# Two softmax attentions: scores two units ahead issued behind the values, maps finished a unit early, output transposes moved ahead of the next values

## The chip, the core and the metric

The kernel runs on one core of one Trainium2 chip. Its time is the device time of one execution, in microseconds (us). The core has a matrix engine (TensorE, PE in the rows, its weight loads PEld), a vector engine (VectorE, DVE), an activation engine (ScalarE, ACT), a general engine (GpSimd, POOL) and a queue that here only issues DMAs (SyncE, SP). Each engine works through its own instructions in the order in which they were written, and semaphores hold an instruction until another engine has done its part. So an instruction that waits also holds all that stands behind it on its engine.

## The reference

Two model blocks over 512 tokens and width 1024. The first (a state-space scan, dilated attention, a gated FFN) is not touched. The second has two layers, and the change is in their attentions and a little around them. Layer A, differential attention with 8 heads; layer B, forgetting attention with 16 heads of 64:

```python
# A: per head, per block of 128 queries, keys up to the block's end
logits = einsum(q[:, q0:q0+128], k[:, :k_end]) + bias      # two maps per head
p = softmax(logits)
attn = p[:, 0] - lam * p[:, 1]
o = rms_norm(einsum(attn, v[:, :k_end]), subln_g) * (1 - lambda_init)
...
# B: c is the running sum of log forget gates
logits = einsum(q[:, q0:q0+128], k[:, :k_end]) + c[t] - c[s]
o = einsum(softmax(where(dist >= 0, logits, NEG_INF)), v[:, :k_end])
...
# after each attention: h = h + rms_norm(f), f = conv_ffn(rms_norm(h))
u = causal_conv_width_3(x @ w_in) + conv_b
gate, val = split(u)
f = (gelu(gate) * val) @ w_out
```

## The kernel before

All large products are float32 to nearly full precision, made from three products of rounded parts (high times high, low times high, high times low). GpSimd splits each slab of weights into its two parts ahead of its use: a slab is two chunks of 128 rows by 256 columns (`whi`, `wlo`), four slabs make a panel of 1024 rows, and four slabs at most are ready ahead. A slab is 12 products of 512 columns on TensorE (L634), or 24 of 256 columns where the result is wanted token by token (the values v2 and v3, L628). The two PSUM banks of a panel are freed when VectorE has copied its result out (`evicted`), called "epi" in the lists below.

Each attention has 32 units, u = 0 to 31: unit u is head tile u//4 and query block u%4, so its width is 128, 256, 384 or 512 keys. The function `order2` (L232) writes one list of steps, and all engines go through that one list, each taking its own part of a step. The steps of a unit:

- S (TensorE, L948): both score maps into AUX banks 0 and 1; waits until VectorE has read the maps of the unit before (`sc_ready`).
- M: VectorE adds the bias and takes the maximum (L2019, L2022), ScalarE does the two exponentials (L1358). In layer B the bias row `negc` comes by DMA from `c_dram`.
- D (VectorE): reciprocals (L2029); in layer A also the difference of the two maps into `dif` (L2033, L2036).
- T: TensorE transposes `dif` (A) or `sc` (B) (L987), ScalarE copies the result to `pT` (L1368), and in B VectorE copies the second half (L2026). T waits until ScalarE has read the last output transpose (`oT_ready`).
- V (TensorE, L1002 in A, L997 in B): values. W: VectorE scales them into `osb2` (L2050 or L2046); in A ScalarE squares them (L1372).
- Y, layer A only, once per tile of four units: ScalarE takes the square root (L1375), which needs another activation table than the exponential, and VectorE normalizes the tile (L2053, L2055).
- X, once per tile: TensorE transposes the tile's output (L968), ScalarE copies it to `oT` (L1378). In the last units O rounds it into `opA_hi` (ScalarE, L1382) and `opA_lo` (VectorE, L1438).

Between these steps stand the slabs of the next pair's q, k and v panels (12 for 8 units), in the last 8 units six slabs of the output projection. Before the change one unit of layer A reads: M(u+1), T(u), S(u+2), W(u-1), D(u+1), slab, V(u), slab. Y and X of a tile come in the second and the third unit of the next tile (u%4 = 1 and 2). Seven products of a mask with an identity (`keep_warm`, L735) stand ahead of T at u = 0, 1, 24 and 25.

Layer B begins with a projection of the forget gates ("f"): narrow transposes, a softplus on ScalarE and VectorE (`sp_step`, ending in L2088), running sums on TensorE (L1031), a copy and a DMA to `c_dram` (L1409), and the load of `negc`. TensorE does three slabs of q3 before it waits for the softplus, and the fourth after the sums.

The FFN of each layer (`fin`, L1924 on) runs over 11 pairs of panels. VectorE copies a panel out of PSUM (L1935), and does two convolution taps per tile (L1945), the product with the gate (L1952) and the low part (L1956).

## Time and profile before

| | us |
|---|---|
| median of 3 runs (2549.43 to 2551.54) | 2551.06 |
| the profiled execution | 2551.49 |
| its span, first to last instruction | 2549.7 |
| TensorE busy | 2484.7 (97%) |
| VectorE busy | 1314.8 (52%) |
| ScalarE busy | 748.1 (29%) |
| GpSimd busy | 1617.3 (63%) |
| mean granted TensorE clock | 0.993 |

Layer A's attention runs from about 1238 to 1443 us of the span, layer B's from about 1899 to 2131. The times of instructions are from one execution. A matmul's recorded time is longer than its share of the engine, since matmuls overlap: 12 products of 512 columns, each recorded with 0.39 us, pass in about 2.8 us. A row's last bracket gives the idle time of the engine just before the instruction and what ended it. Where the granted clock is 1.00 the matrix engine runs at its upper level, 2.4 GHz; where it is 0.50 at the lower one, 1.2 GHz.

### The profile page before, as it was taken

Reading aid. Unit: us, or ns where it says so; the run is one execution under the profiler, and the core shown is the slowest. Engines: PE = TensorE matmul, PEld = TensorE weight load, DVE = VectorE, ACT = ScalarE, POOL = GpSimd, SP = SyncE. Lnnn points to the kernel's source line nnn. Section 1 sums busy time; section 2 is a strip of 40 time slices with the busy share of each in tenths; the row PEclk is TensorE's granted clock in tenths of the full one; section 3 lists DMA queues with packets and bytes.
Section 4 is the critical chain, followed back from the end, with each engine's and each line's share of the span. In section 5 each row is a group of like instructions: output and inputs, shape, how many; then the busy total and the mean of one; then the engine's idle time right before and its main releaser. Section 6 shows DMA issues by size and latency. Waiting matters only on the chain. (4 is left out here: it accounts for less than half of the span.)

```text
span 2549.7 us, 37097 instructions
## 1 busy us (share of the span) xinstructions
PE 2484.7 (97%) x12731; PEld 2054.1 (81%) x12744; DVE 1314.8 (52%) x2044; ACT 748.1 (29%) x1396; POOL 1617.3 (63%) x1548
## 2 busy tenths in 40 slices
PE   9999999999999999999999899999989999999998
PEld 7888898888778888888787677888867777878886
DVE  8778675435226333302555468773173344787722
ACT  3564551011232111102244434331032222433300
POOL 8765666755447777776543368887653324778874
PEclk9999999999999999999999999999999999999999
DMA  5433434322224333332321123333222212333331
GB/s 163 128 101 92 114 100 133 97 71 71 67 66 124 96 98 95 96 98 83 105 65 58 50 83 93 97 95 100 78 85 71 71 59 66 84 90 98 95 99 62
DMA packets 235792, 229.22 MB, mean 90 GB/s; under 512 B 15809, under 2 KB 228289, under 8 KB 235673
## 3 DMA queue, kind: packets, MB, share of 16 engines
q1 hardware_dynamic: 212224, 204.72, 28.0%
q10 hardware_dynamic: 23448, 22.84, 3.0%
q8 instruction: 83, 1.36, 0.2%
q14 instruction: 37, 0.30, 0.0%
HBM read 225.29 MB, written 4.84 MB: 90 GB/s over the span
## 5 line engine op out<-in xcount | busy, mean ns | idle before, releaser
L594 POOL TENSOR_TENSOR wlo<-raw,whi 128x512 fp32r<-128x512 f32 x772 | 1056.7, 1369 | 64.5
L592 POOL TENSOR_SCALAR whi<-raw 128x512 fp32r<-128x512 f32 x772 | 562.4, 728 | 841.8 <-issue 446.9
L634 PE MATMUL PS<-opA_hi,whi 128*128 128x512 f32 x1872 | 745.0, 398 | 11.8 <-DVE fu L1935 4.3
L634 PE MATMUL PS<-opA_hi,wlo 128*128 128x512 f32 x1872 | 730.9, 390 | 0.0
L634 PE MATMUL PS<-opA_lo,whi 128*128 128x512 f32 x1872 | 730.3, 390 | 0.0
L634 PEld LDWEIGHTS PS<-opA_hi,whi 128*128 128x128 f32 x1872 | 352.6, 188 | 98.7 <-issue 14.9
L634 PEld LDWEIGHTS PS<-opA_hi,wlo 128*128 128x128 f32 x1872 | 352.1, 188 | 75.0
L634 PEld LDWEIGHTS PS<-opA_lo,whi 128*128 128x128 f32 x1872 | 352.8, 188 | 70.3 <-issue 1.2
L1945 DVE SCALAR_TENSOR_TENSOR facc<-fu,vec,facc 128x512 f32<-128x512 f32 x176 | 206.2, 1230 | 44.9 <-ACT facc L1330 44.6
L628 PE MATMUL PS<-whi,opA_hi 128*128 128x256 f32 x704 | 205.7, 292 | 0.0
L628 PE MATMUL PS<-wlo,opA_hi 128*128 128x256 f32 x704 | 198.9, 283 | 0.0
L628 PE MATMUL PS<-whi,opA_lo 128*128 128x256 f32 x704 | 198.9, 283 | 0.0
L634 PE MATMUL PS<-hid_hi,whi 128*128 128x512 f32 x480 | 186.7, 389 | 0.0
L634 PE MATMUL PS<-hid_lo,whi 128*128 128x512 f32 x480 | 186.7, 389 | 0.0
L634 PE MATMUL PS<-hid_hi,wlo 128*128 128x512 f32 x480 | 186.7, 389 | 0.0
L628 PEld LDWEIGHTS PS<-whi,opA_hi 128*128 128x128 f32 x704 | 134.6, 191 | 7.5 <-issue 4.7
L628 PEld LDWEIGHTS PS<-whi,opA_lo 128*128 128x128 f32 x704 | 134.7, 191 | 1.4 <-issue 1.2
L628 PEld LDWEIGHTS PS<-wlo,opA_hi 128*128 128x128 f32 x704 | 134.6, 191 | 0.0
L1900 DVE COPY branch<-PS 128x512 f32<-128x512 f32 x32 | 21.0, 687 | 210.0 <-PE PS L634 147.9
L1358 ACT ACTIVATE sc<-sc,bstat 128x128 f32<-128x128 f32 (+3 forms) x128 | 70.8, 554 | 117.3 <-DVE bstat L2022 117.3
L634 PEld LDWEIGHTS PS<-hid_hi,wlo 128*128 128x128 f32 x480 | 90.1, 188 | 18.8
L634 PEld LDWEIGHTS PS<-hid_hi,whi 128*128 128x128 f32 x480 | 90.1, 188 | 18.7
(306 smaller groups left out, 3310.7 us busy)
## 6 DMA issues: line engine op xcount, KB each, us to landing
raw<-in_w_in_dram SPq DMA_DIRECT2D x184, 256.0 KB, 2.8
raw<-in_ffn_w_in_dram SPq DMA_DIRECT2D x176, 256.0 KB, 2.7
raw<-in_ffn_w_out_dram SPq DMA_DIRECT2D x88, 256.0 KB, 2.8
raw<-in_a_w_qkv_dram SPq DMA_DIRECT2D x48, 256.0 KB, 2.7
raw<-in_w_ffn_gate_dram SPq DMA_DIRECT2D x44, 256.0 KB, 2.8
raw<-in_w_ffn_up_dram SPq DMA_DIRECT2D x44, 256.0 KB, 2.7
raw<-in_w_ffn_down_dram SPq DMA_DIRECT2D x44, 256.0 KB, 2.9
acs_row<-acs_dram ACTq DMA_DIRECT2D x16, 512.0 KB, 5.6
```

The source lines that it names most:

```text
L592: nc.gpsimd.tensor_scalar(whi[slot][:], raw[raw_slot][:], 1.0, 1.0, ALU.mult, ALU.mult).then_inc(w_high, 1)
L594: nc.gpsimd.tensor_tensor(wlo[slot][:], raw[raw_slot][:], whi[slot][:].bitcast(F32), ALU.subtract).then_inc(slab_split, 1)
L628: last = nc.tensor.matmul(psum_tm(key, panel)[:, t, :], a, b[:, c, :], start=t % 2 == 0 and k + n == 0, stop=k == total - 1 and n == 2, sk ...
L634: last = nc.tensor.matmul(psum_fm(key, panel, m), a, b[:, k, :], start=k + n == 0, stop=k == total - 1 and n == 2)
L1358: A(sc[:, u % 2, e, 0:width], sc[:, u % 2, e, 0:width], ACT.Exp, bias=bstat[:, u % 4, 2 + e:3 + e], accum_out=bstat[:, u % 4, 4 + e:5 + e] ...
L1900: V.tensor_copy(branch[:, c, :], psum_fm(key, c // 2, c % 2)).then_inc(evicted, 1)
L1945: V.scalar_tensor_tensor(facc[:, j, :], fu[:, j, tap:tap + S], col("ffn_conv_w_2", 132 * l + 44 * tap + FT * half + m + 2 * i), facc[:, j, ...
```

## The change

- `order2` is rewritten. One unit of layer A now reads: T(u), D(u+1), slab, V(u), W(u), S(u+2), M(u+2), slab. So the scores of u+2 stand behind the values of u, and the exponentials of u+2 stand ahead of the copy to `pT` of u+1. The two halves of the old step Y are now Y (ScalarE's square root, behind W of the tile's last unit) and Z (VectorE's normalization, behind D(u+1) of the next unit); the two halves of O are O and L. X stands directly ahead of V of the next tile's first unit, and in layer A it waits for Z.
- X also waits for the copy of the transposes just ahead of it, since it stands behind T now.
- The first two slabs of the next pair stand between S(0) and S(1).
- `keep_warm` is issued at u = 24 and 25 only.
- In layer B all four slabs of q3 stand ahead of the running sums, TensorE's wait for `c_ready` is at T(0), and the copy of v3 out of PSUM stands ahead of the softplus on VectorE.
- In `fin`, VectorE copies the next pair's first panel out between the taps of the two halves.
- ScalarE does one small copy at the very start.

```diff
--- before.py
+++ after.py
@@ -232,49 +232,45 @@
 def order2(names):
     project = "awo" if names[0] == "q2" else "bwo"
-    out = [("S", 0), ("S", 1), ("M", 0), ("D", 0)]
-    late = []
+    out, late = [("S", 0), ("M", 0), ("D", 0)], []
     for j in range(PAIRS):
         fill = [("slab", (n, j + 1), 0, h) for n in names for h in range(4)] if j < PAIRS - 1 else []
-        for n in range(9, len(fill) + 3, 2):
+        if j == 0:
+            out += fill[:2] + [("S", 1), ("M", 1)]
+            fill = fill[2:]
+        for n in range(9 - 2 * (j == 0), len(fill) + 3, 2):
             fill.insert(n, None)
         if j == PAIRS - 1:
             fill = [None] * 2 + [("slab", project, n, k) for k in range(3) for n in range(2)]
         for u in range(8 * j, 8 * j + 8):
-            if u < 31:
-                out.append(("M", u + 1))
-            out += [("W", u - 1)] * (u > 0 and names[0] == "q3") + [("T", u)]
-            if u < 30:
-                out.append(("S", u + 2))
-            out += [("W", u - 1)] * (u > 0 and names[0] != "q3")
+            done = u // NB - 1
+            out.append(("T", u))
             if u < 31:
                 out.append(("D", u + 1))
+            if u % NB == 0 and u and names[0] == "q2":
+                out.append(("Z", done))
+            if u > 24:
+                out.append(("L", u - 25))
             out += late
             late = []
-            done = (u - 5) // NB
-            if u % NB == 1 and u > NB and names[0] == "q2":
-                out.append(("Y", done))
             for part in ("V", "X"):
-                if part == "X" and u % NB == 2 and u > NB:
-                    out.append(("X", done))
                 if fill and (j < PAIRS - 1 or part == "X"):
                     t = fill.pop(0)
                     out += [t] * (t is not None)
                     if t is not None and t[1] != project and t[3] == len(K1024) - 1:
                         late = [("epi", t[1], t[2])]
                 if part == "V":
-                    out.append(("V", u))
+                    out += [("X", done)] * (u % NB == 0 and u > 0) + [("V", u), ("W", u)]
+                    if u % NB == NB - 1 and names[0] == "q2":
+                        out.append(("Y", u // NB))
+                    if u < 30:
+                        out += [("S", u + 2), ("M", u + 2)]
             if u in range(24, 31):
                 out.append(("O", u - 24))
-    return out + [("W", 31)] + [("Y", 7)] * (names[0] == "q2") + [("X", 7), ("O", 7)]
+    return out + [("Z", 7)] * (names[0] == "q2") + [("X", 7), ("O", 7), ("L", 7)]
 WEIGHTS = ["w_in", "w_ssm_out", "w_att_out", "w_mix_out", "w_ffn_gate", "w_ffn_up", "w_ffn_down", "a_w_qkv_2", "a_w_o_2", "w_kvf_2",
            "b_w_q_2", "b_w_o_2", "ffn_w_in_2_0", "ffn_w_in_2_1", "ffn_w_out_2_0", "ffn_w_out_2_1"]
@@ -429,7 +425,7 @@
         AUX = ctx.enter_context(nc.psum_tensor("AUX", [P, 4, S], F32))
         x_in = [sem(f"x_in{n}") for n in range(4)]
-        warm_ready = sem("warm_ready")
+        warm_ready, table_ready = sem("warm_ready"), sem("table_ready")
         first_in, const_in = sem("first_in"), sem("const_in")
         w_loaded = [sem(f"w_loaded{n}") for n in range(RAW)]
         slab_go, w_high, slab_split = sem("slab_go"), sem("w_high"), sem("slab_split")
@@ -962,8 +958,10 @@
                     elif kind == "X":
                         if fox:
                             pe.wait_ge(o2_read, 32 + 8 * (u + 1))
+                            pe.wait_ge(pT2_dve, min(NB * u + NB + 1, 32))
                         else:
                             pe.wait_ge(o2_normed, u + 1)
+                            pe.wait_ge(pT2_act, min(NB * u + NB + 1, 32))
                         for n in range(NB):
                             last = nc.tensor.transpose(AUX[:, 2 + fox, n * P:(n + 1) * P], osb2[:, u % 2, n, :], ident[:])
                         last.then_inc(ot2_done, 1)
@@ -974,7 +972,9 @@
                         U = u_base + u
                         if kind == "T":
                             wait(pe, oT_ready, tiles)
-                            if u % (8 * (PAIRS - 1)) < 2:
+                            if fox and u == 0:
+                                pe.wait_ge(c_ready, 1)
+                            if u in (24, 25):
                                 keep_warm(WARM_UNIT, 2 + fox)
                             if fox:
                                 wait(pe, exp2, 2 * U + 2)
@@ -1021,8 +1021,7 @@
             twin_mm(("k3", 0), 7)
             factors_between(7, ("v3", 0), 0)
             narrow_transposes("f", f_rows, BH)
-            for k in range(3):
-                slab(("q3", 0), 0, k)
+            panel_mm(("q3", 0), 0)
             pe.wait_ge(sp_step, 33)
             for t in range(NB):
@@ -1030,8 +1029,6 @@
                 for n, (part, x) in enumerate(sums):
                     last = nc.tensor.matmul(AUX[0:BH, 2, t * P:(t + 1) * P], x, part[:], start=n == 0, stop=n == len(sums) - 1)
             last.then_inc(c_done, 1)
-            slab(("q3", 0), 0, 3)
-            pe.wait_ge(c_ready, 1)
             attention(("q3", "k3", "v3"), 1)
             for n in range(2):
                 slab("bwo", n, 3)
@@ -1080,6 +1077,9 @@
                 A(std[:], AUX[:, 3, 0:NB], ACT.Sqrt, bias=EPS, scale=1.0 / D).then_inc(std_ready, 1)
+            act.wait_ge(warm_ready, 1)
+            A(std[:], rstd_bc[:, 0:NB], ACT.Copy).then_inc(table_ready, 1)
+            act.wait_ge(table_ready, 1)
             act.wait_ge(first_in, 16 * N_FIRST)
             for c in range(DC):
                 act.wait_ge(x_in[c // 2], 16)
@@ -1969,9 +1969,9 @@
                 evict(1, 1)
                 with dve.Fori(1, FP - 1) as i:
                     taps(i, 0)
-                    taps(i, 1)
                     dve.wait_ge(fconv_tap, 88 * l + 8 * i + 4)
                     evict(i, 0, 1)
+                    taps(i, 1)
                     products(i)
                     evict(i, 1, 1)
                 taps(FP - 1, 0)
@@ -2035,7 +2035,7 @@
                             wait(dve, tr2_done, u - 1)
                             V.scalar_tensor_tensor(dif[:, u % 2, 0:width], sc[:, u % 2, 1, 0:width], st[:, 10:11], sc[:, u % 2, 0, 0:width],
                                                    ALU.mult, ALU.add).then_inc(r2_step, 1)
-                    elif kind == "O":
+                    elif kind == "L":
                         low(opA_lo[:, u, :], oT[:, u, :], None, opA_hi[:, u, :])
                     elif kind == "W":
                         wait(dve, ot2_done, 8 * fox + tile - 1)
@@ -2048,7 +2048,7 @@
                         else:
                             dve.wait_ge(pv2_done, u + 1)
                             V.tensor_scalar(osb2[:, tile % 2, qb, :], AUX[:, 3, 0:P], st[:, 6:7], None, ALU.mult).then_inc(o2_read, 1)
-                    elif kind == "Y":
+                    elif kind == "Z":
                         dve.wait_ge(o2_std, u + 1)
                         V.reciprocal(ostat[:, u % 2, 2 * NB:3 * NB], ostat[:, u % 2, NB:2 * NB]).then_inc(o2_rstd, 1)
                         dve.wait_ge(o2_rstd, u + 1)
@@ -2082,11 +2082,11 @@
             opB_low(7)
             scale_first(("k3", 0), k_first)
             narrow_columns(fx, bfv[:], 2, BH)
+            qkv2(("v3", 0))
             step, q, a = softplus((fa, fe, fr, fz, fz2, fq), 18, 3)
             step(V.scalar_tensor_tensor(fz[:], q[:], 2.0, a[:], ALU.mult, ALU.add))
             step(V.tensor_tensor(fr[:, 2, :], fz[:, 0, :], fz[:, 1, :], ALU.add))
             step(V.tensor_tensor(fr[:, 3, :], fr[:, 2, :], fz[:, 2, :], ALU.add))
-            qkv2(("v3", 0))
             qkv2(("q3", 0))
             softmax_units(("q3", "k3", "v3"), 1)
             residual("bwo", 8, "b_norm_post_2", 0, ("ffn_norm_pre_2", 8), 2, (("fin", 1), fu_first))
```

In the instruction streams of the engines this looks as follows. The first place is ScalarE in layer A, where the first tile has ended: the square root with its table (L1375), the exponentials (L1358), the copies to `pT` (L1368), the squares (L1372) and the copy of the transposed output (L1378). Before:

```order
L1372 ACTIVATE osq,ostat<-osb_164 128x128
L1375 ACT_TABLE_LOAD
L1375 ACTIVATE ostat<-ostat 128x4
L1358 ACT_TABLE_LOAD
L1358 ACTIVATE sc,bstat<-sc,bstat 128x512 x2
L1368 ACTIVATE pT<-AUX 128x384
L1372 ACTIVATE osq,ostat<-osb_164 128x128
L1378 ACTIVATE oT<-AUX,subg 128x512
```

and now:

```order
L1372 ACTIVATE osq,ostat<-osb_164 128x128
L1375 ACT_TABLE_LOAD
L1375 ACTIVATE ostat<-ostat 128x4
L1358 ACT_TABLE_LOAD
L1358 ACTIVATE sc,bstat<-sc,bstat 128x256 x2
L1368 ACTIVATE pT<-AUX 128x128
L1378 ACTIVATE oT<-AUX,subg 128x512
```

The square root stood one unit and more behind the tile's last square and three instructions ahead of the output copy; now it follows the last square directly, and the output copy comes after one exponential and one copy to `pT`.

The same place on VectorE: reciprocals (L2029), the difference (L2033, L2036), the normalization (L2053, L2055) and the scaled values (L2050). Before:

```order
L2029 RECIPROCAL bstat<-bstat 128x2
L2033 TENSOR_SCALAR bstat<-bstat,lams 128x1
L2036 SCALAR_TENSOR_TENSOR dif<-sc,bstat 128x384
L2053 RECIPROCAL ostat<-ostat 128x4
L2055 TENSOR_TENSOR osb_164<-osb_164,ostat 128x512
```

and now:

```order
L2029 RECIPROCAL bstat<-bstat 128x2
L2033 TENSOR_SCALAR bstat<-bstat,lams 128x1
L2036 SCALAR_TENSOR_TENSOR dif<-sc,bstat 128x256
L2053 RECIPROCAL ostat<-ostat 128x4
L2055 TENSOR_TENSOR osb_164<-osb_164,ostat 128x512
L2050 TENSOR_SCALAR osb_164<-AUX,bstat 128x128
```

The normalization now stands behind the difference of width 256, whose exponentials follow the two table loads above; before it stood behind the difference of width 384, whose exponentials came before them.

On TensorE, the output transposes (the x4 row) and what is around them. Before:

```order
L628 MATMUL PS<-whi_59,opA_lo 128x256
L628 MATMUL PS<-wlo_63,opA_hi 128x256
L1002 MATMUL AUX<-v_0_158,pT 128x128 x3
L968 MATMUL AUX<-ident,osb_164 128x128 x4
L987 MATMUL AUX<-ident,dif 128x128 x4
L948 MATMUL AUX<-k_1_157,q_1_155 128x256 x2
```

and now (the numbers of lines are four or two lower there for the same code):

```order
L624 MATMUL PS<-wlo_62,opA_hi 128x256
L966 MATMUL AUX<-ident,osb_164 128x128 x4
L1002 MATMUL AUX<-v_0_158,pT 128x128
L944 MATMUL AUX<-k_0_156,q_0_154 128x384 x2
L987 MATMUL AUX<-ident,dif 128x128 x2
```

They stood behind the values of the next tile's third unit and stand now ahead of the values of its first, and the scores follow the values.

## Rows read from the trace of the kernel before

**Rows 1.** Busy time by stretch, layer A's attention: length, engines, clock, DMA share, GB/s.

```profile
1238.00:1440.00 202.00, 187.42 (x1062) 146.25 (x1065) 108.29 (x337) 88.32 (x258) 80.03 (x84) 0.97 0.18 54
```

**Rows 2.** Waits of TensorE around layer A's attention: waiter, awaited, us, times, longest.

```profile
PE AUX L1002 <- ACT pT L1368: 6.0, 4, 3.8
PE AUX L948 <- DVE bstat L2019: 4.5, 2, 3.1
PE AUX L987 <- ACT oT L1378: 2.3, 3, 0.8
```

**Rows 3.** The same view around layer B's attention.

```profile
PE AUX L987 <- DVE osb L2046: 7.2, 9, 1.5
...
PE AUX L987 <- ACT oT L1378: 2.1, 3, 0.7
```

**Rows 4.** ScalarE in time order, layer A: start us, us, engine, line, operation.

```profile
1328.87 0.30 ACT L1372 ACTIVATE osq<-osb 128x128 f32<-128x128 f32 x1
...
1329.28 1.28 ACT L1375 ACT_TABLE_LOAD   x1
1330.58 0.20 ACT L1375 ACTIVATE ostat<-ostat 128x4 f32<-128x4 f32 x1
1330.80 1.28 ACT L1358 ACT_TABLE_LOAD   x1
...
1341.36 0.51 ACT L1358 ACTIVATE sc<-sc,bstat 128x256 f32<-128x256 f32 x1 [0.95 <-DVE bstat L2022]
```

**Rows 5.** VectorE in time order, layer A.

```profile
1331.03 0.69 DVE L2055 TENSOR_TENSOR osb<-osb,ostat 128x512 f32<-128x512 f32 x1
...
1344.20 0.35 DVE L2050 TENSOR_SCALAR osb<-AUX,bstat 128x128 f32<-128x128 f32 x1 [2.87 <-PE AUX L1002]
1344.46 0.16 DVE L2029 RECIPROCAL bstat<-bstat 128x2 f32<-128x2 f32 x1
...
1344.96 0.67 DVE L2036 SCALAR_TENSOR_TENSOR dif<-sc,bstat 128x256 f32<-128x256 f32 x1
```

**Rows 6.** The chain that ended last: seven mask products, a slab, a slab of values.

```profile
1913.34 1.53 PE AUX L735 x7
1916.58 2.82 PE PS L634 x12
...
1941.67 2.93 PE PS L628 x24
```

**Rows 7.** TensorE in time order, layer A: scores of width 256.

```profile
1316.79 0.70 PE L948 MATMUL AUX<-k,q 64*128 64x256 f32 x4
```

**Rows 8.** Widest maps, layer A: one of two bias passes, one of two exponentials.

```profile
1304.74 0.68 DVE L2019 CUSTOM_DVE_ANT_0 sc<-AUX,tbias 128x512 f32<-128x512 f32 x1
...
1405.09 0.72 ACT L1358 ACTIVATE sc<-sc,bstat 128x512 f32<-128x512 f32 x1 [1.18 <-DVE bstat L2022]
```

**Rows 9.** Busy time by stretch, columns as in rows 1: TensorE's clock after idle time.

```profile
1402.00:1404.00 2.00, 0.00 (x0) 0.00 (x0) 1.84 (x4) 1.89 (x3) 0.00 (x0) 1.00 0.00 0
1404.00:1406.00 2.00, 0.80 (x4) 0.50 (x4) 1.28 (x6) 0.91 (x3) 0.00 (x0) 0.53 0.00 0
...
1432.00:1434.00 2.00, 2.00 (x10) 1.90 (x10) 0.12 (x1) 0.35 (x1) 0.00 (x0) 0.50 0.00 0
```

**Rows 10.** The start of layer B's attention in time order.

```profile
1901.42 0.29 DVE L2019 CUSTOM_DVE_ANT_0 sc<-AUX,negc 128x128 f32<-128x128 f32 x1 [2.08 <-DMA negc<-c_dram]
...
1901.99 0.79 PE L948 MATMUL AUX<-k,q 64*128 64x256 f32 x4 [1.84 <-DVE bstat L2019]
...
1905.88 0.39 PE L987 MATMUL AUX<-ident,sc 128*128 128x128 f32 x2
```

**Rows 11.** The first FFN's second pair of panels, VectorE and TensorE in time order.

```profile
1541.89 4.93 DVE L1945 SCALAR_TENSOR_TENSOR facc<-fu,vec,facc 128x512 f32<-128x512 f32 x4 [2.49 <-ACT facc L1330]
...
1548.27 0.47 PE L634 MATMUL PS<-opA_hi,whi 128*128 128x512 f32 x1 [2.14 <-DVE fu L1935]
```

**Rows 12.** TensorE at the kernel's start.

```profile
11.18 0.51 PE L634 MATMUL PS<-opA_hi,whi 128*128 128x512 f32 x1 [0.18 <-POOL wlo L594]
```

## The prediction

> **What bounds the kernel now.** I read the page first: TensorE is busy for 97% of the span, so only its idle time and its clock can be won, some 65 us in all. The waits of TensorE say where that time lies, and the stretches say how much of it the two attentions hold: layer A's attention has 202.0 - 187.4 = 14.6 us of idle time at a mean clock of 0.97 [rows 1]. In A the longest waits are for the copies to `pT` and for the maps ahead of scores [rows 2]; nearly all lie in the last 8 units, where few slabs are left to cover a chain over three engines. In the 24 units before them TensorE waits only 0.8 us per two tiles, for the copy of the output. In B it waits for the scaled values (8 times 0.72 us in the body, once 1.5 in the end) and for the output copy [rows 3]. Then I went through the instructions in time order, for the price of each step, and walked the new list by hand, one engine beside the other, with these prices.
>
> **The prices.** Square 0.41 (start to the next load), first table load to second 1.52, second load 1.28, exponentials of width 256 about 1.1 (two of 0.5 with their sums) [rows 4]. Scaled values 0.35, reciprocal to difference 1.17, normalization 0.69 and about 0.2 for its reciprocal [rows 5]. A slab 2.82, a slab of values 2.93, seven mask products 1.5 [rows 6]. Scores of width 256 hold TensorE 0.6, the widest 1.1 [rows 7]. Widest maps: 1.5 on VectorE, 1.5 on ScalarE [rows 8].
>
> **Layer A, the body.** X of a tile now waits for Z, Z stands behind D(u+1) on VectorE, D(u+1) waits for the exponentials of u+1, and these follow both table loads on ScalarE. From the end of V of a tile's last unit: hand-over 0.1, W 0.35, square 0.41, load to load 1.52, load 1.28, exponentials 1.10, difference 1.17, normalization 0.90, further hand-overs 0.15: 6.98 us until X can start. Meanwhile TensorE has S 0.63, T 0.2 and one slab of 2.93, 3.8 in all: a wait of 3.2 us. That is tile 0. At tile 1 VectorE copies a value panel out ahead of W (4.1); tile 3 gives 3.3; at tiles 2 and 4 a second slab leaves 0.4 each. Sum 11.4. Besides, V of a unit now waits for a copy to `pT` that stands behind the exponentials of the next unit: 1.9 once and three times 0.4, 3.1 in all. Removed: three waits of 0.8 for the output copy [rows 2] and 0.3 of small ones. Body: 11.4 + 3.1 - 2.6 = +11.9. Queued behind X are V, the next scores and all slabs, so nothing covers this.
>
> **Layer A, the end.** Before, the waits from u = 25 on sum to 11.9 us, most of them in [rows 2]. Now X of tile 5 has no slab ahead of it, only S, T and the mask products: 6.98 - 2.5 = 4.5. X of tile 6 has one: 3.3. Where no slab stands between, V(u) to V(u+1) takes the widest scores 1.1, the map 1.5, the exponentials 1.5 [rows 7, 8], the rounding for the output and a copy, about 5.5, against 1.6 of TensorE's own work: 3.9 at the worst, 2.2 at V(25) behind the mask products, and 0.7 to 1.2 at four others, with 0.8 at the last X, 10.4 in all. Sum 18.2, so +6.3.
>
> **Layer A, the entry.** Scores of unit 0 start as before, at 1238.0. T(0) came 5.7 us later; now S 0.4, two slabs and S(1) 0.6 make 6.6, with no wait. +0.9, two slabs fewer later (-5.6), and no mask products at T(1) (-1.5): -6.2.
>
> **The clock.** After 2 us without any matmul, and little before, the granted clock falls from 1.00 to 0.5 [rows 9]. It did so twice in A's end, for about 7 and about 3.5 us, which is 3.4 and 1.7 us of work lost. The change makes six idle stretches of 3.2 us or more, three in the body. I take 1.5 for each of the three, since slabs follow, and 1.1 for each of the three in the end, where TensorE waits anyway: 7.8 against 5.1 before, +2.7. The unknown has as ends nothing (-5.1) and 3.4 each (+15.3).
>
> Layer A: 11.9 + 6.3 - 6.2 + 2.7 = **+14.7**.
>
> **Layer B.** The fourth slab of q3, 2.82 us [rows 6], goes into the wait for the softplus, which is a little shorter; the running sums start 0.3 later, and the load of `negc` with them. The copy of v3, 1.7 us, goes into VectorE's wait for ScalarE's first exponential, at no cost; if it did not fit it would be 1.7. The first map starts when `negc` has landed, 1901.42 before and 1901.7 now, and frees S(1) at 1902.3, against 1901.99 [rows 10]. S(1) takes 1.0, and T(0) comes at 1903.4 instead of 1905.9, since no mask products stand ahead of it: -2.5. The two slabs between S(0) and S(1) cover the load of `negc` but for 0.5 and are done by then, -5.6. The mask products of T(1) go: -1.5. In the body 5.8 of 0.72s and 2.1 of output copies go [rows 3], 2.1 come back as waits for `pT`: -5.7. There is no Z here, so X waits only for copies. In the end the waits rise from about 5 to about 9.5 by the chain of layer A's end: +4.5, and one of them, 3.7, should cost a clock step: +1.7. Layer B: **-9.1**.
>
> **The FFN.** VectorE's copy came behind two pairs of taps, the second of which is 4.93 us, and TensorE waited 2.14 us for it, once in each FFN [rows 11]. Now it falls into VectorE's own wait of 2.49. In the later pairs the copy must wait for TensorE's panel with the taps behind it; VectorE has about 5 us of slack in the 22 of a pair, and TensorE needs the result one panel later. -4.3, bounds -4.3 and 0.
>
> **The start.** The early copy takes the table load off the way to the first matmul. TensorE's second slab still waited for GpSimd [rows 12], so what is won comes back as that wait: -0.1, bounds -1.3 and 0.
>
> **The sum.** 14.7 - 9.1 - 4.3 - 0.1 = +1.2, so 2552.7 by the profiled execution's 2551.49. This is 0.4 above the median of the runs; by the median it is 2552.3, and I say 2552.5.
>
> What counts as a change that can be told from none is 0.2% of the time, 5.1 us.
>
> One rule speaks against this change. The two loads around the square root cost 1.52 us from the start of one to the start of the other, and the square root itself starts 1.30 after the first load's start [rows 4]. The Trainium skill (ScalarE: Activation LUTs, What ACT_TABLE_LOAD costs) puts 1283 ns for the load and about 1380 ns for a drain on every switch. By that rule two switches in each of seven chains, of which before only the last was exposed, would add an estimated 17 to 19 us, and the sum would be near 2571. The trace does not agree: no drain stands between load and square root.
>
> **The rivals.**
>
> *The clock decides (slower).* Each of the six stretches costs what the first one before did, 3.4 us, instead of 1.3: +12.6, 2565. For it: in [rows 9] the lower level outlasted the wait by 4 us, and at half speed the engine's small steps in A's end are late for the next chain too. Against it: in the body slabs follow at once. From 2.0 us a stretch on, the kernel is slower by more than 0.2%.
>
> *The normalization is not what X waits for (faster).* V of the same unit waits for a copy behind the same exponentials, 5.1 us after the last V, so 1.3 of wait stay in any case. If Z were through by then, as when D is not in its way, five waits shrink by 1.9 and the clock mostly stays up: -9.5 and about -1.5, 2541.5. For it: before, Z came between two maps without holding anyone. Against it: Z now stands behind D of width 256, which needs the exponentials behind the loads.
>
> *Layer B's entry gives nothing (slower).* The load of `negc` or the split weights are late, TensorE waits out what the two slabs should cover: +5.6, 2558. For it: `negc` was 2.1 us late for VectorE [rows 10]. Against it: TensorE waited there for vectors and loads alone, for no weights, and GpSimd may be four slabs ahead.
>
> *The change does not do what it says.* The maps are a unit early only by their place; if the chain through them sets the pace in the body as well, every unit with one slab loses about 1 us, 12 in A and B each, 2575. V's small waits of 0.4 in my walk bound this from below.
>
> **The numbers.** Forecast 0.42, the clock 0.28, the normalization 0.20, B's entry 0.06, the pace of the chain 0.04. The forecast's own range is 2546 to 2558, and its upper tail beyond 2556.2 counts as slower. Faster 0.22, same 0.42, slower 0.36. The range 2542 to 2566 leaves out the third loss and half of the gain's tail.
>
> **What would show it.** In the changed trace: waits of TensorE at the output transposes for VectorE's normalization, seven of them in A, near 3, 4, 0.4, 3, 0.4, 4.5 and 3 us; half clock after the long ones; no wait at T in the body of either attention; T(0) of B 2.5 us earlier, counted from the sums, with two slabs ahead of it; no wait on L1935. The forecast is wrong if the waits at X are under 1.5 us, or if the clock's share in A is above 12 us, or if B gains under 5.

## The result and the profile after

The changed kernel takes 2561.25 us (median of 5 runs, 2560.33 to 2564.17), the kernel before 2551.53 us on the same chip. The ratio is 1.0043, 95% interval [1.0029, 1.0057]: the change costs 9.7 us. The forecast was 2552.5.

I cut both executions at the same three instructions: the first scores of layer A's attention, its last output transposes, and the last output transposes of layer B's. The view is busy time by stretch, with the columns of [rows 1]. Before:

```profile
core 0: us, PE busy (x) PEld busy (x) DVE busy (x) ACT busy (x) POOL busy (x), PEclk, DMA share, GB/s
1238.03:1442.71 204.68, 189.49 (x1071) 147.56 (x1073) 109.13 (x339) 90.01 (x261) 80.45 (x85) 0.97 0.19 55
1442.71:2130.24 687.53, 663.21 (x3422) 539.99 (x3427) 355.96 (x620) 193.97 (x352) 424.71 (x400) 1.00 0.28 82
2130.24:2549.70 419.46, 404.68 (x1799) 331.98 (x1799) 239.98 (x255) 113.89 (x149) 303.77 (x278) 0.98 0.30 87
```

The same three stretches of the changed kernel:

```profile
1238.01:1464.23 226.22, 195.95 (x1057) 150.45 (x1059) 106.87 (x339) 92.34 (x261) 83.99 (x85) 0.93 0.16 50
1464.23:2144.09 679.86, 662.58 (x3410) 543.64 (x3414) 373.34 (x620) 192.89 (x352) 424.07 (x400) 0.99 0.27 83
2144.09:2559.50 415.41, 402.73 (x1799) 330.75 (x1799) 254.72 (x255) 113.92 (x149) 302.64 (x278) 0.99 0.29 88
```

| stretch | forecast | measured | TensorE's idle time | its busy time |
|---|---|---|---|---|
| layer A's attention | +14.7 | +21.5 | +15.1 | +6.5 |
| first FFN and layer B | -11.2 | -7.7 | -7.0 | -0.6 |
| second FFN | -2.1 | -4.1 | -2.1 | -2.0 |

The spans differ by 9.8 us, and the three rows add up to it. Read the last two columns together. In A the changed kernel has 14 instructions of TensorE fewer (mask products, some 4.1 us of it), and is busy 6.5 us longer all the same: the engine ran at its lower clock for longer.

Where A waits now (waits of TensorE, columns of [rows 2]):

```profile
PE AUX L966 <- DVE osb L2055: 19.2, 8, 4.4
PE AUX L1002 <- ACT pT L1368: 9.5, 10, 3.6
PE AUX L1002 <- issue: 1.5, 2, 1.0
```

The first row is new. It is the output transposes waiting for the normalization, at 3.31, 3.64, 0.37, 3.31, 0.36, 4.35, 3.19 and 0.64 us in order of time. The forecast had 3.2, 4.1, 0.4, 3.3, 0.4, 4.5, 3.3 and 0.8. The waits of scores for `bstat` and of the map's transposes for `oT` [rows 2] are gone.

The forecast's chain can be read off in tile 5, in time order over three engines:

```profile
1405.98 0.35 DVE L2050 TENSOR_SCALAR osb<-AUX,bstat 128x128 f32<-128x128 f32 x1 [1.68 <-PE AUX L1002]
...
1406.36 0.31 ACT L1372 ACTIVATE osq<-osb 128x128 f32<-128x128 f32 x1 [2.48 <-DVE osb L2050]
...
1406.78 1.28 ACT L1375 ACT_TABLE_LOAD   x1
1408.08 0.21 ACT L1375 ACTIVATE ostat<-ostat 128x4 f32<-128x4 f32 x1
1408.30 1.28 ACT L1358 ACT_TABLE_LOAD   x1
1409.60 0.51 ACT L1358 ACTIVATE sc<-sc,bstat 128x256 f32<-128x256 f32 x1
...
1410.72 0.17 DVE L2029 RECIPROCAL bstat<-bstat 128x2 f32<-128x2 f32 x1 [3.19 <-ACT sc L1358]
...
1411.63 0.17 DVE L2053 RECIPROCAL ostat<-ostat 128x4 f32<-128x4 f32 x1
1411.84 0.69 DVE L2055 TENSOR_TENSOR osb<-osb,ostat 128x512 f32<-128x512 f32 x1
...
1412.58 1.11 PE L966 MATMUL AUX<-ident,osb 128*128 128x128 f32 x4 [4.35 <-DVE osb L2055]
```

From the scaled values to the transposes it is 6.60 us, of which 2.82 is from the start of the first table load to the end of the second. VectorE sits idle for 3.19 us with the normalization queued behind the difference. The square root starts 1.30 us after its load, as in [rows 4]: no drain. The Trainium skill (ScalarE: Activation LUTs, What ACT_TABLE_LOAD costs) has a drain of about 1380 ns with every switch; the trace after does not show it either, and the 2571 us that would follow from it were not reached.

What the forecast had wrong shows in the clock behind such waits, by stretch:

```profile
1300.00:1304.00 4.00, 2.39 (x10) 1.38 (x10) 1.83 (x5) 1.09 (x3) 0.12 (x1) 0.76 0.24 70
1304.00:1308.00 4.00, 4.00 (x17) 3.04 (x16) 2.11 (x8) 1.31 (x4) 0.00 (x0) 0.82 0.00 0
...
1356.00:1360.00 4.00, 2.94 (x11) 1.44 (x11) 1.96 (x6) 1.09 (x3) 0.00 (x0) 0.58 0.19 65
1360.00:1364.00 4.00, 4.00 (x12) 3.18 (x11) 2.27 (x8) 1.30 (x4) 0.00 (x0) 0.56 0.00 0
...
2104.00:2108.00 4.00, 2.88 (x14) 2.76 (x14) 0.86 (x2) 1.07 (x4) 0.00 (x0) 0.52 0.00 0
2108.00:2112.00 4.00, 4.00 (x16) 3.13 (x17) 1.16 (x7) 1.40 (x5) 0.00 (x0) 0.62 0.00 0
```

The first two pairs are in layer A, the third in B. 4 us times the missing share of the clock gives (0.24 + 0.18) x 4 = 1.7 us for the first pair, 3.4 for the second and for the third. Over A six stretches add up to 15.4 us (1.7, 1.7 and 3.4 in the body, 3.4, 3.4 and 1.7 in the end) where the kernel before had 6.8 in three. This sum also counts time in which TensorE stood idle at the lower level, and lost no work. Weighted with its busy share in steps of 0.5 us, it is 13.5 against 5.6.

In layer B (waits of TensorE from 1905 us on):

```profile
PE AUX L997 <- ACT pT L1368: 4.4, 2, 3.4
PE AUX L997 <- DVE pT L2026: 3.7, 5, 0.9
PE AUX L997 <- issue: 1.7, 2, 1.2
PE AUX L944 <- DVE bstat L2019: 1.5, 1, 1.5
PE AUX L966 <- DVE pT L2026: 0.9, 2, 0.5
PE AUX L987 <- ACT sc L1358: 0.9, 1, 0.9
```

The 7.2 us at the scaled values and the 2.1 at the output copies of [rows 3] are gone; at the values (L997) 9.8 us stand where there were 2.6.

### The profile page after: what moved, and what is told of

The parts are those of the page before. It is cut to its first block, busy times and chain, and to the rows that moved or that the text cites. A ratio compares the mean times of both kernels' runs of the same rounds, so it can differ in the third digit from the quotient of the medians.

```text
span 2559.5 us, 37062 instructions
## 1 busy us (share of the span) xinstructions
PE 2488.7 (97%) x12705; PEld 2059.3 (80%) x12716; DVE 1344.5 (53%) x2044; ACT 749.8 (29%) x1397; POOL 1620.0 (63%) x1548
## 4 chain that ended last, share of the span: by engine, by line
PE 87%; DVE 6%; ACT 4%; issue 2%; DMA 0%; ACTq 0%; DVEq 0%
PE PS L630 64%; PE PS L624 9%; PE PS L703 3%; PE AUX L944 2%; PE AUX L997 1%; DVE opA_lo L1440 1%; PE AUX L910 1%; PE AUX L891 1%; ACT opA_hi L1073 1%; PE AUX L987 1%; PE AUX L848 1%; DVE XT L1920 1%; PE AUX L1002 1%; ACT sc L1358 1%; PE AUX L737 0%
## 5 line engine op out<-in xcount | busy, mean ns | idle before, releaser
L630 PEld LDWEIGHTS PS<-opA_hi,whi 128*128 128x128 f32 x1872 | 353.1, 189 | 96.9 <-issue 13.2
L1945 DVE SCALAR_TENSOR_TENSOR facc<-fu,vec,facc 128x512 f32<-128x512 f32 x176 | 216.7, 1289 | 15.8 <-ACT facc L1330 15.8
L1358 ACT ACTIVATE sc<-sc,bstat 128x128 f32<-128x128 f32 (+3 forms) x128 | 70.9, 555 | 184.1 <-DVE bstat L2022 184.0
L630 PEld LDWEIGHTS PS<-hid_lo,whi 128*128 128x128 f32 x480 | 90.1, 188 | 18.7
```

The source lines that it names most:

```text
L630: last = nc.tensor.matmul(psum_fm(key, panel, m), a, b[:, k, :], start=k + n == 0, stop=k == total - 1 and n == 2)
L1358: A(sc[:, u % 2, e, 0:width], sc[:, u % 2, e, 0:width], ACT.Exp, bias=bstat[:, u % 4, 2 + e:3 + e], accum_out=bstat[:, u % 4, 4 + e:5 + e] ...
L1945: V.scalar_tensor_tensor(facc[:, j, :], fu[:, j, tap:tap + S], col("ffn_conv_w_2", 132 * l + 44 * tap + FT * half + m + 2 * i), facc[:, j, ...
```

## The experiments

The ratios are to the kernel before, timed beside each experiment, whose median was 2550.4 to 2550.9 us.

**One part back: layer A in the old order.** The changed kernel with the old list for layer A alone, and the mask products at units 0 and 1 there.

```diff
 def order2(names):
     project = "awo" if names[0] == "q2" else "bwo"
+    if names[0] == "q2":
+        return order2_old(names)
...
-                            if u in (24, 25):
+                            if u in (24, 25) or not fox and u < 2:
```

> Layer A's attention takes the order of before (with the mask products at units 0 and 1), all else is the changed kernel. Theory (the loss sits in A alone: its attention took 21.5 us longer, from scores of unit 0 to the last output transpose, while B and the two FFNs gained): the time falls by 21.5, from 2561.3 to about 2539.8, 11.7 under the kernel before. Rival (part of the loss comes from outside A's attention, from the clock or from weights that are late elsewhere): over 2545.

Measured: 2539.35 us (2538.35 to 2539.98), ratio 0.9955 [0.9941, 0.9968]. So layer A's new order costs 21.9 us, and all else in the change wins 11.5 (their difference is 10.4 and not 9.7, since the kernel before was 0.7 lower beside this run). The sign of the whole is decided in one attention.

**The idle time filled.** The changed kernel with mask products, read by nobody, ahead of the first seven output transposes of layer A: 14, 14, 2, 14, 2, 18 and 14.

```diff
+                            if u < 7:
+                                pe.wait_ge(o2_read, NB * (u + 1))
+                                keep_warm((14, 14, 2, 14, 2, 18, 14)[u], 3)
                             pe.wait_ge(o2_normed, u + 1)
```

> The changed kernel, with mask products into a free bank ahead of each of the first seven output transposes of A (14 each where the wait was over 3 us, 18 at tile 5, 2 at tiles 2 and 4), so that the matrix engine has work while it waits. The waits for the normalization keep their length. Theory (each long wait costs a stretch at half clock of 3.4 or 6.8 us besides, 1.7 to 3.4 us of work, and this comes on top of the wait): the granted clock stays at 1.00 in the body of A, and the time falls by 7 to 10, to 2551 to 2554. Rival (the slow stretches lie beside other waits and cost little): 2559 to 2562.

Measured: 2554.14 us (2552.30 to 2557.75), ratio 1.0016 [1.0007, 1.0025], 7.1 less than the changed kernel though nothing that TensorE waits for comes earlier. Layer A's attention:

```profile
PE AUX L1005 <- ACT pT L1371: 10.8, 10, 3.6
PE AUX L969 <- DVE osb L2058: 2.2, 6, 0.7
...
sum 218.51, PE 203.07 PEld 152.84 DVE 109.28 ACT 92.25 POOL 83.82; mean PE 203.07 PEld 152.84 DVE 109.28 ACT 92.25 POOL 83.82
```

Idle time falls from 30.3 to 15.4, and 78 mask products at the 0.219 us each of [rows 6] add 17.1; yet the engine's busy time rises by only 7.1. The other 10.0 us are the lower clock that was avoided. The mechanism held; the time is a tenth above the range expected of it.

**The transposes later.** X of layer A one unit later, ahead of the values of the next tile's second unit.

```diff
-                    out += [("X", done)] * (u % NB == 0 and u > 0) + [("V", u), ("W", u)]
+                    out += [("X", done)] * (u % NB == late_x and u > NB - 1) + [("V", u), ("W", u)]
...
-                            pe.wait_ge(pT2_act, min(NB * u + NB + 1, 32))
+                            pe.wait_ge(pT2_act, min(NB * u + NB + 2, 32))
```

> The changed kernel with A's output transposes one unit later (ahead of the values of the tile's second unit, u%4 = 1, instead of the first). The square root, its tables and the normalization stay where they are. Theory (the output transposes wait for the normalization behind the difference behind the table loads; a unit later the 7.0 us chain is over): the seven waits of 19.2 in all go, V of the first unit keeps a wait of about 1.3 us for its copy where one slab stands ahead, 5 in all, and the clock stays up in the body: 14 + 7 less, about 2540. Rival (the new place of scores and maps sets the pace by itself, the transposes only show it): the wait moves to the values, 2550 or more.

Measured: 2554.59 us (2553.28 to 2555.88), ratio 1.0014 [1.0005, 1.0023]. The time is the rival's (2550 or more), 14 us above the theory's. No wait at X for the normalization is left but 0.7 us at the last tile, yet the waits have moved to the values: those for `pT` sum to 13.2, and two more appear at the values of units 16 and 24, one 4.93 and one 5.97 us. Around the first, in time order:

```profile
1349.45 0.69 DVE L2056 TENSOR_TENSOR osb<-osb,ostat 128x512 f32<-128x512 f32 x1
1350.06 1.65 DVE L1706 TENSOR_SCALAR v<-PS,rstd_col 128x256 f32<-128x256 f32 x4
...
1351.81 0.76 PE L1003 MATMUL AUX<-v,pT 128*128 128x128 f32 x2 [4.93 <-issue]
```

The trace names no releaser, but VectorE's copy of the value panel out of PSUM ends at 1351.71, and the values, which need that panel, start 0.10 later. In its list the copy stands behind the normalization, and so behind the same two table loads. The next experiment tests this.

**The copy ahead.** As the last, and the copy of a panel stands ahead of the difference.

```diff
+            if late_x:
+                out += late
+                late = []
             if u < 31:
                 out.append(("D", u + 1))
```

> As e3_x_late (the output transposes of the first attention a unit later), and the copy-out of the value panels stands ahead of the next unit's masks' division in VectorE's list, not behind it. Theory (the waits of 4.9 and 6.0 us at the 16th and 24th unit's values in e3_x_late came from that copy-out, which stood behind the division and so behind the two table loads): both waits go, and with them their clock: 2554.6 - 10.9 - about 4 = 2540. Rival: those values wait for something else, or the division now comes late for the transposes: 2550 or more.

Measured: 2544.54 us (2541.64 to 2546.05), ratio 0.9973 [0.9964, 0.9983]. Both waits are gone, and the time is 10.1 us less; in the traces layer A has 10.5 less (220.1 to 209.6). The cause was right, the size expected (2540) was not reached. Layer A is still 6.5 us longer than in the first experiment (203.1). It now waits here:

```profile
PE AUX L1006 <- ACT pT L1372: 16.6, 13, 3.6
PE AUX L970 <- ACT pT L1372: 3.3, 3, 2.1
```

The copies to `pT` stand behind the next unit's exponentials. Waits for them sum to 6.0 before [rows 2], to 19.9 here; in return some 7 us of the old order's waits, for `bstat` and `oT` [rows 2], are gone. No experiment changes the place of the exponentials alone, so how this remainder divides stays open. Nor was the normalization tried ahead of the difference, the nearest cure for the 19.2 us.

**No table to switch.** The changed kernel with a square in place of the square root in layer A's second attention. It leaves the root out of the normalization.

```diff
-                        A(ostat[:, u % 2, NB:2 * NB], ostat[:, u % 2, 0:NB], ACT.Sqrt, bias=SUB_EPS, scale=1.0 / P).then_inc(o2_std, 1)
+                        A(ostat[:, u % 2, NB:2 * NB], ostat[:, u % 2, 0:NB], ACT.Square, scale=1.0 / P).then_inc(o2_std, 1)
```

> The changed kernel, with the square root of A's normalization replaced by a square, so that no activation table is loaded between the exponentials. It leaves the square root out. Theory (the loads are 2.6 of the 7.0 us chain, no drain besides): waits at the output transposes of 3.3 become 0.7, 4.4 becomes 1.8, the short ones go, 19.2 becomes 5; with the clock up, about 22 less, 2539. Rival (a switch costs a drain of some 1.4 us each besides, as the Trainium skill has it): the chain is 5.3 shorter, no wait is left there, and about 27 is won, 2534.

Measured: 2545.62 us (2539.93 to 2547.55), ratio 0.9976 [0.9965, 0.9986]. Layer A's attention:

```profile
PE AUX L1002 <- ACT pT L1368: 9.6, 10, 3.6
PE AUX L966 <- DVE osb L2055: 7.5, 5, 2.3
...
1238.19:1444.64 206.45, 187.27 (x1057) 145.48 (x1059) 109.53 (x339) 73.47 (x246) 85.61 (x84) 0.98 0.18 54
```

This is the cleanest comparison of the study. TensorE issues the same 1057 instructions as in the changed kernel; its idle time is 11.1 us less, and its busy time 8.7 us less. So here 1 us less of waits brought 0.8 more in clock. The time came out 6.6 us above what I expected, for two reasons. Each long wait at the transposes shrank by only 1.9 to 2.4 us, so 7.5 are left and not 5; tile 5's, 4.35 in the changed kernel, is the longest. And this execution, 19.8 us shorter in layer A, is only 16.0 shorter in all: up to the last output transposes of B TensorE is busy 3.6 us longer, with the clock down also from 1476, 1845 and 1957 us on, behind waits of only 0.19, 0.19 and 1.06. The times fall in two groups, two runs near 2540 and six at 2545 to 2548. The rival's drains did not show: the waits shrank by less than the 2.8 us of the two loads, not by 5.3.

```profile
1397.44 0.65 PE L966 MATMUL AUX<-ident,osb 128*128 128x128 f32 x4 [2.33 <-DVE osb L2055]
```

So at this tile the rest of the chain, some 4.2 us, is by itself longer than the work that TensorE has beside it.

**The FFN alone.** The kernel before, with its copy between the taps.

```diff
                     taps(i, 0)
-                    taps(i, 1)
                     dve.wait_ge(fconv_tap, 88 * l + 8 * i + 4)
                     evict(i, 0, 1)
+                    taps(i, 1)
```

> The kernel before with one edit alone: in the feed-forward stages the eviction that follows the last product's group is put between the taps, and so the two stages' ends no longer wait 2.14 us on the last hidden rows. My theory: each of the two stages gets shorter by 2.1 to 2.2 us (it did in the changed kernel: 2.15 and 2.1), so -4.3 us, about 2547. Rival: the stage's end is hidden behind something else that is late when it comes earlier, the time stays at 2551 (above 2550).

Measured: 2544.43 us (2542.41 to 2548.84), ratio 0.9979 [0.9969, 0.9989]: 5.9 us less, more than the two waits. In the changed kernel the second FFN is shorter by 4.1 us for one wait of 2.13. The execution of the kernel before shows what can come on top, around that wait, which ended at 2236.85 (busy time by stretch):

```profile
2234.00:2238.00 4.00, 1.87 (x7) 1.25 (x6) 4.00 (x5) 0.09 (x1) 3.08 (x3) 0.87 0.20 66
2238.00:2242.00 4.00, 4.00 (x14) 3.11 (x14) 3.62 (x6) 3.80 (x5) 0.38 (x1) 0.70 0.21 66
```

The clock fell there: (0.13 + 0.30) x 4 = 1.7 us. In the first FFN it stayed at 1.00 after a wait of 2.14 [rows 11], and that FFN's share was 2.1, as forecast. That the 1.6 us beyond the forecast, in the median of runs from 2542 to 2549, are this clock is likely but not shown by one execution.

**Layer A's entry alone.** The first experiment with the change's start of layer A: two slabs between S(0) and S(1), no mask products.

```diff
-    out = [("S", 0), ("S", 1), ("M", 0), ("D", 0)]
+    out = [("S", 0), ("M", 0), ("D", 0)]
...
+        if j == 0:
+            out += fill[:2] + [("S", 1)]
+            fill = fill[2:]
```

> e1_a_old (the first attention in the order of the kernel before, all else changed) with the changed kernel's beginning of that attention: two slabs of the value weights' products between the first two scores, no mask products there. Theory (the entry's term of the forecast, -6.2 with clock, of which part was lost to the clock): 2539.4 - 4 = about 2535. Rival: the gap at the entry comes back at the first transposes, 2539 or more.

Measured: 2535.76 us (2534.70 to 2537.40), ratio 0.9942 [0.9929, 0.9956]: 3.6 us below the first experiment and the fastest kernel of the study, 15 us below the one before and 25 below the changed one. From the first scores to T(1) it takes 14.41 us against 12.86, with two more slabs (5.6) done: 4.1 us won. The forecast had 6.2 for this. It read the entry off an execution in which the clock was low there; with the same old list, the first experiment has it at 1.00. This kernel has the changed one's entry, so it prices the rest of the new order: 25.5 us in the times, 24.9 in A (226.2 against 201.3), and 8.3 of it are left with the copy ahead (209.6).

**Layer B's slab back.** The first experiment with the slab of q3 where it was before: three slabs, the sums, the fourth slab. All else that the change does at layer B's start stays: the copy of v3, the place of S(1), and no mask products.

```diff
-            panel_mm(("q3", 0), 0)
+            for k in range(3):
+                slab(("q3", 0), 0, k)
...
             last.then_inc(c_done, 1)
+            slab(("q3", 0), 0, 3)
```

> e1_a_old with the second attention's beginning as in the kernel before: three slabs, the sums, then the fourth slab, in place of all that the change does there. Theory (the first transposes wait less for the map behind the slab, forecast at -2.5 us in the changed kernel): 2539.4 + 2.5 = about 2542. Rival: the place of the slab is worth nothing, since the scores' wait for the statistics (1.5 us) takes its place: 2539.4 within 1 us.

Measured: 2539.67 us (2538.46 to 2542.23), ratio 0.9955 [0.9941, 0.9968], 0.3 from the first experiment, whose runs overlap with these. The rival was right: moving the slab is worth nothing that can be measured. The traces show how. With the slab back TensorE waits 2.46 us ahead of the sums and 1.45 ahead of S(0); in the first experiment it waits 1.45 for `bstat` at S(1) and 0.98 for the exponentials at T(0), 1.5 less in all. But there the clock is at 0.76 and 0.82 between 1900 and 1908 us, 1.7 us of work, while it stays at 1.00 with the slab back.

**The end kept busy.** The fastest kernel (layer A's entry alone) with 12 mask products ahead of the scores of unit 28 and 16 ahead of the values of unit 30 of layer A.

```diff
+                        if u == 28 and not fox:
+                            pe.wait_ge(o2_read, 26)
+                            keep_warm(12, 3)
                         scores(u)
...
+                            if u == 30 and not fox:
+                                pe.wait_ge(o2_read, 30)
+                                keep_warm(16, 3)
```

> e7_a_old_entry with products that nobody reads in the two long idle stretches near the end of the first attention: 12 mask products ahead of the scores of unit 28, which waited 3.07 us, and 16 ahead of the values of unit 30, which waited 3.83 us. At 0.21 us each they last 2.5 and 3.4 us and fit into the waits. Theory (an idle stretch costs its own length and then some 1.7 to 3.4 us of work at the lower clock): the waits' ends stay, the clock stays at 1.00 in both places, and the time falls by about 4 to 5 us, from 2535.8 to about 2531. Rival (the clock falls anyway, or the lower clock costs nothing because the work behind it is hidden): 2535 or more.

Measured: 2537.62 us (2537.09 to 2538.49), ratio 0.9949 [0.9936, 0.9963], 1.9 slower than without them. A miss, and a telling one. TensorE around unit 30 without the products:

```profile
1423.34 0.49 PE L1031 MATMUL AUX<-ident,dif 128*128 128x128 f32 x3
1427.65 1.20 PE L1046 MATMUL AUX<-v,pT 128*128 128x128 f32 x6 [3.83 <-ACT pT L1412]
...
1433.25 0.60 PE L1031 MATMUL AUX<-ident,dif 128*128 128x128 f32 x4
```

and with them:

```profile
1423.61 0.49 PE L1034 MATMUL AUX<-ident,dif 128*128 128x128 f32 x3
1426.25 3.63 PE L775 MATMUL AUX<-mask,ident_bf 128*128 128x512 bf16 x16 [2.15 <-DVE osb L2100]
1429.71 0.83 PE L1052 MATMUL AUX<-v,pT 128*128 128x128 f32 x6
...
1433.58 0.60 PE L1034 MATMUL AUX<-ident,dif 128*128 128x128 f32 x4
```

The products had to wait for their bank, 2.15 us, and so ran past the end of the wait: the values start 2.06 us later. But 4 us on, at the next transposes, only 0.33 of this is left, 0.27 of which was there before: the clock, at 1.00 from 1428 to 1432 us against 0.57 without the products, gave back 1.7. At unit 28 they came after 3.54 us of idle time, at half clock, and took 4.45. From the transposes ahead of them to the next it is 12.84 us, against 11.81 without: 1.0 lost. The clock's price is confirmed, the filling as placed is not worth it.

## Why the prediction was off, point by point

The forecast's signs held for all three stretches but not its sizes, and the time, 2561.25, lies outside the forecast's own range (2546 to 2558) and within the wide one, which takes in most of what the clock was thought able to cost. Of the three outcomes, the one given 0.36 came (slower by more than 0.2%), not the one given 0.42. The time is nearer to the rival in which the clock decides (2565) than to the forecast (2552.5). One of the prediction's own signs of being wrong appeared: the clock's share in A above 12 us (15.4, or 13.5 where only busy time counts). The other two did not.

- *The body and the end of A: right.* The waits at the transposes sum to 19.2 us against 20.0 by the walk, and those at the values to 11.0 against 12.7. All idle time of A rose by 15.1 us; the terms of the forecast, without clock and mask products, give 16.0.
- *The clock's term of A: the step that failed.* +2.7 was forecast. Measured is the rise of busy time, 6.5, and the 4.1 of mask products that went: about +10.5 (by the stretches with a low clock it is 8.6, or 7.9 weighted with busy time). The average over the six stretches is 15.4 / 6 = 2.6 us, where I took 1.5 and 1.1 (7.8 in all), on the argument that slabs follow in the body and that TensorE waits anyway in the end. The runs show neither saves: in the body 1.7, 1.7 and 3.4 us were lost with slabs right behind, in the end 3.4, 3.4 and 1.7, of which 2.5, 3.0 and 1.7 are busy time. The prediction named 2.0 as the point from which the kernel is slower by more than 0.2%. Two experiments show that this is clock and not work: 10.0 us came back with the idle time filled, and 8.7 with waits 11.1 us shorter (no switch).
- *The entry of A: too large.* -6.2 forecast; alone it gives -4.1 by the trace and -3.6 by the times.
- *Layer B: right in sign, too large.* It won 5.5 us (7.7 less 2.1 of the FFN) against 9.1, and 5.1 by the medians of the FFN experiment and the first. T(0) came 11.2 us after the sums, 12.5 before: -1.3 for -2.5, since S(1) waited 1.5 and not 0.5. The waits in body and end fell by 1.5, forecast 1.2. The other 2.7 us missing fit the clock: its two drops at 2092 and 2104 us make 5.1, forecast were 1.7. No experiment isolates this.
- *The FFN: right in the wait, too small in all.* Both waits of 2.1 went, and with the second 1.9 us of busy time; -6.2 for -4.3.
- *The start: not to be told.* The first scores of A start at 1238.0 in both, but at 1236.8 to 1239.4 in the experiments, most of which have the same instructions up to there. The -0.1 forecast is far below that spread.
- *The rivals.* That the normalization is not what X waits for is refuted by the wait's row. That the pace of the chain takes 1 us a unit did not occur: in A's body the values wait at only five units, and at three of them for 0.2 us. Layer B's entry gave nothing for its slab, but the two slabs between S(0) and S(1) there were not tried apart from the rest.

Not settled: what decides whether the clock falls after a wait under 3 us.

## What to carry to other kernels

Before a consumer is moved up, walk its producer's queue on each engine: a normalization that is ready in time stands late when it is queued behind work that waits for two table loads. Price an idle stretch of TensorE of 3 us or more at its length and, by these traces, another 1.7 or 3.4 us for the lower clock after it, and don't discount that because work follows at once. And take a change apart: all that lies outside layer A's order won 11.5 us here, and that order lost 21.9. The fastest kernel, at 2535.76 us, keeps the parts that win.

## What the runs showed of the hardware that was not expected

The same instructions with the same waits met different clocks. The old start of layer A has TensorE idle for 0.53, 1.40 and 0.2 to 0.3 us. In the execution of the kernel before the clock fell in it:

```profile
1240.00:1244.00 4.00, 3.67 (x13) 1.43 (x14) 1.79 (x10) 1.97 (x8) 0.00 (x0) 0.57 0.22 66
```

and in that of the first experiment it did not:

```profile
1241.00:1245.00 4.00, 3.30 (x16) 1.53 (x18) 2.03 (x12) 1.72 (x7) 0.06 (x1) 1.00 0.23 66
```

Six mask products passed in 2.54 us there and in 1.30 here. Waits of 2.14 and 2.13 us in the two FFNs cost 0 and 1.7 us of clock. A wait of 2.45 us ahead of layer B's sums cost nothing in the kernel before and 1.7 in the FFN experiment, whose instructions there are the same. And behind a wait of only 0.19 us in the second FFN the clock fell in both kernels, from 2162 and from 2176 us on, at 1.7 us of work each. So one profile's clock behind a short wait is one draw, 1.7 us wide, and a term read from it should carry that width. After each wait of 3.06 us and more in the two attentions, in all eleven traces, the clock was at its lower level within 2 us.
